# One tile first: the other tiles' first block with tile 0's expert rows between its instructions

## The reference, cut to what matters

```python
h = rms_norm(x, g_mix)
p = h @ w_in                                   # 672 columns for attention, 1792 for the recurrence
y_a = mla_group(p[..., :672], ...)             # w_uq, w_uk, w_uv, norm of q and k, chunk mask, 8 heads
y_r = rwkv7_group(p[..., 672:], ...)           # lora, a state of 64x64 for each of 8 heads, token by token
x = x + concat(y_a, y_r) @ w_o
h = rms_norm(x, g_ffn)
q = (h @ w_pq).reshape(T, 8, 2, 128)           # expert layer, for each block of 128 tokens
s = einsum('thpd,hpnd->thpn', q, sub_keys)
s1, i1 = top_k(s[:, :, 0], 16); s2, i2 = top_k(s[:, :, 1], 16)
top_s, pos = top_k(s1[..., :, None] + s2[..., None, :], 16)    # of the 256 sums
idx = take(i1 * 128 + i2, pos); gate = softmax(top_s)
act = gelu(einsum('thkd,td->thk', expert_u[idx], h))
x = x + einsum('thk,thkd->td', gate * act, expert_v[idx])      # 8 heads x 16 = 128 rows a token
```

## Time and profile before

| what | value |
| --- | --- |
| median of 3 runs | 2452.07 us (2451.54 to 2456.14) |
| profiled execution: span, first to last instruction | 2444.8 us |
| the median less this span | 7.3 us |
| busy: TensorE, VectorE, ACT, GpSimd | 85%, 63%, 48%, 30% of the span |
| moved by DMA | 721.34 MB, mean 295 GB/s |
| granted TensorE clock, mean of the span | 0.910 of full |

### The profile page before, as it was taken

The page is one execution under the profiler, slowest core; times in us unless marked ns, Lnnn a source line. Parts: engine busy times, 40 slices in busy tenths (PEclk is TensorE's granted clock), DMA queues, the critical chain, the costliest instruction groups (busy, mean ns, idle before and its releaser), DMA issues.

```text
span 2444.8 us, 34688 instructions
## 1 busy us (share of the span) xinstructions
PE 2077.5 (85%) x13276; PEld 1613.4 (66%) x13276; DVE 1544.6 (63%) x3434; ACT 1181.8 (48%) x2346; POOL 739.4 (30%) x647
## 2 busy tenths in 40 slices
PE   6989999888868765666659899876998999989998
PEld 4445598678656654555558788755887756858863
DVE  5565676677887746667566787556766544955422
ACT  1123332127776567666676567768776640111110
POOL 2000000004444334555543796333333310800000
PEclk9999879999979987666679999987999999999999
DMA  4321113549999999999999999999999985353441
GB/s 168 121 100 64 70 37 107 182 145 400 421 418 418 415 415 420 422 419 418 415 419 416 412 381 409 414 419 415 400 413 412 411 319 206 112 178 116 167 143 69
DMA packets 158437, 721.34 MB, mean 295 GB/s; under 512 B 10048, under 2 KB 13248, under 8 KB 92224
## 3 DMA queue, kind: packets, MB, share of 16 engines
q0 software_dynamic: 73728, 536.90, 53.5%
q1 hardware_dynamic: 84544, 182.23, 20.5%
HBM read 717.00 MB, written 2.10 MB: 294 GB/s over the span
## 4 chain that ended last, share of the span: by engine, by line
PE 47%; DMA 27%; DVE 13%; ACT 7%; issue 4%; POOL 3%; another core or an unknown queue 0%; SPq 0%; DVEq 0%; POOLq 0%; ACTq 0%
DMA AR<-in_uv,C 24%; PE PA L684 12%; PE PD L1213 8%; PE PA L1146 5%; PE PD L684 5%; ACT AR L1749 3%; PE PA L1159 3%; DVE AR L2635 2%; DMA WR<-in_w_up 2%; POOL AR L2825 2%; PE PD L847 2%; PE PA L1314 2%; PE PD L1314 2%; PE PA L847 1%; DVE AR L2579 1%
## 5 line engine op out<-in xcount | busy, mean ns | idle before, releaser
L2579 DVE CUSTOM_DVE_ANT_0 AR<-AR,HN 128x1024 f32<-128x1024 f32 x512 | 639.6, 1253 | 406.8 <-DMA AR<-in_uv,C 217.3
L2825 POOL DMA_INDIRECT AR<-in_uv,C x512 | 617.4, 1206 | 918.2 <-PE PD L1213 723.0
L1213 PE MATMUL PD<-C,AR 128*128 128x128 f32 x4096 | 653.4, 313 | 279.3 <-ACT AR L1749 278.1
L1213 PEld LDWEIGHTS PD<-C,AR 128*128 128x128 f32 x4096 | 549.9, 162 | 415.1 <-ACT AR L1749 369.0
L1749 ACT ACTIVATE AR<-AR,SC 128x1024 f32<-128x1024 f32 x512 | 588.2, 1149 | 16.7
L1745 ACT ACTIVATE SC<-SC 128x1 f32<-128x1 f32 x512 | 103.3, 202 | 352.1 <-DVE SC L2579 350.7
L684 PE MATMUL PA<-HT,WR 128*128 128x256 f32 (+1 forms) x608 | 185.2, 465 | 1.4 <-ACT AR L1763 1.4
L1146 PE MATMUL PA<-HT,WR 128*128 128x256 f32 x704 | 170.3, 389 | 11.7 <-DMA WR<-in_w_up 11.7
L684 PEld LDWEIGHTS PA<-HT,WR 128*128 128x128 f32 x608 | 116.3, 192 | 64.8 <-issue 55.0
L1747 ACT ACTIVATE SC<-SC,C 128x1 f32<-128x1 f32 x512 | 150.8, 295 | 16.6
L1146 PEld LDWEIGHTS PA<-HT,WR 128*128 128x128 f32 x704 | 131.8, 196 | 28.9 <-DMA WR<-in_w_up 13.3
(11 more groups left out here) (488 smaller groups left out, 2895.4 us busy)
## 6 DMA issues: line engine op xcount, KB each, us to landing
WR<-in_w_up SPq DMA_DIRECT2D x22, 2048.0 KB, 18.3
WR<-in_w_in SPq DMA_DIRECT2D x18, 2048.0 KB, 8.0
WR<-in_w_ada SPq DMA_DIRECT2D x12, 2048.0 KB, 8.3
WR<-in_w_down SPq DMA_DIRECT2D x9, 2048.0 KB, 8.8
WR<-in_w_pq SPq DMA_DIRECT2D x4, 2048.0 KB, 28.8
AR<-in_uv,C POOLq DMA_INDIRECT x512, 14.9
WR<-in_w_out SPq DMA_DIRECT2D x4, 2048.0 KB, 18.1
AR<-in_w_pq SPq DMA_DIRECT2D x3, 2048.0 KB, 10.1
```

The costliest lines, as they stand in the source:

```text
L1213: ins = nc.tensor.matmul(acc[i // 4][:, P * (i % 4):P * (i % 4) + P], uv_row(j, D + P * i, D + P * i + P), ident, start=(k == 0 and i % 4 ...
L2579: ttr(uv_row(j, 0, D), uv_row(j, 0, D), HN[:, t, :], 1.0, 0.0, ALU.mult, ALU.add, DOT[:, j:j + 1]).then_inc(s["dots"], 1)
L2825: nc.gpsimd.indirect_dma_start(uv_row(ring_slot(turn), 0, 2 * D), None, uv, bass.IndirectOffsetOnAxis(ap=IDX[:, t % 2, i:i + 1], axis=0),) ...
```

## The change

The head is run twice: head(FIRST) for tile 0 alone, with tile 0's queries, scores and selection part 0 behind it, and then head(LATE, cut) for tiles 1 to 3. In the second one, 128 places are marked by cut(name); at the k-th, VectorE does the product of tile 0's row k, ACT scales row k-1 and TensorE adds row k-2. Tile 0's selection parts 1 to 3 stand at the late head's beginning (the 18 cuts "sel"), tile 1's part 0 near its end. After the late head TensorE adds what is left of tile 0's rows, and the loop over tiles starts with tile 1, whose rows take over what stood between tile 0's: selection parts 1 to 3 (now tile 1's), the mixing of tiles 2 and 3, their queries (rows 29 to 68) and scores, and tile 2's selection from row 77.

```diff
 def ring_slot(turn):
-    if turn < SEVEN:
-        return turn % 5
-    return (turn - SEVEN) % 7 if turn < EIGHT else (turn - EIGHT) % RING
+    return (0, 1, 8, 9)[turn % 4] if turn < NSEL else turn % RING
...
+BREAKS = [name for name, count in
+          (("sel", 18), ("pm", 3), ("q", 6), ("qkn", 9), ("qkT", 2), ("att", 26), ("lora", 8), ("inv0", 3), ("inv", 15),
+           ("invz", 1), ("chain", 6), ("e1", 2), ("e2", 4), ("e3", 2), ("e4", 2), ("e5", 4), ("e6", 4), ("e7", 13))
+          for _ in range(count)]
...
+            ACC0 = [PA[:, 3, :], PD[:, 3, :]]
+            def first_row(k):
+                j = ring_slot(k)
...
+                pe.wait_ge(s["scaled"], k + 1)
+                for i in range(KD):
+                    ins = nc.tensor.matmul(ACC0[i // 4][:, P * (i % 4):P * (i % 4) + P],
+                                           uv_row(j, D + P * i, D + P * i + P), ident,
...
+            def cut(name, count=1):
+                for _ in range(count):
+                    cuts[0] += 1
+                    if cuts[0] > LAG:
+                        first_row(cuts[0] - 1 - LAG)
...
+            head(FIRST, no_cut)
+            w_mix = head(LATE, cut)
...
+            for k in range(rows_done[0], NSEL):
+                first_row(k)
...
+            def scaled_row(t, k):
...
+                act.wait_ge(s["dots"], turn_ + 1)
+                tell(A(GEL[:, j:j + 1], DOT[:, j:j + 1], ACT.Gelu), "gelu")
...
+            def cut(name, count=1):
+                for _ in range(count):
+                    if cuts[0] > 0:
+                        scaled_row(0, cuts[0] - 1)
+                    cuts[0] += 1
...
+            def product_row(turn_, t):
+                j = ring_slot(turn_)
+                dve.wait_ge(uv_full[j], 16 * ring_uses(turn_))
...
+            def cut(name, count=1):
+                for _ in range(count):
+                    product_row(cuts[0], 0)
+                    cuts[0] += 1
...
-            for t in range(NT):
+            for t in range(1, NT):
                 for k in range(NSEL):
...
+                    if turn == NSEL:
+                        pool.wait_ge(s["a_full"], JA["score", 1, 3] + 1)
```

More of the change, by code:

```diff
@@ L95 @@
 LAG = 2
[L96 to L99, removed]
+MIX_NORM_AT = {2: (5, 8, 11, 14), 3: (16, 18, 21, 23)}
+MIX_TURN_AT = {2: 17, 3: 26}
+QUERY_FROM, QUERY_TO = 29, 68
+SCORE_AT = 70
 def select_at(t):
[L104 removed]
+    return [77 + 5 * i // 4 for i in range(STEPS)] if t == 2 else [15 + 3 * i for i in range(STEPS)]
 GATES_AT = 124
@@ L142, with bank_before @@
 FIRST_A, FIRST_D = {}, {}
-_a = _d = 0
 for _name, _na, _nd in JOBS:
-    FIRST_A[_name], FIRST_D[_name] = _a, _d
-    _a, _d = _a + _na, _d + _nd
-PR_EARLY, PR_IN_ATT = 6, 12
-def pr_after(u):
-    m = PR_EARLY + (u - 2) // 3
-    return m if (u - 2) % 3 == 0 and PR_EARLY <= m < PR_IN_ATT else None
[L160 to L208, removed]
+    FIRST_A[_name], FIRST_D[_name] = len(BANK_A), len(BANK_D)
+    for _i in range(_na):
+        add_a(_name, _i, "late")
+    for _i in range(_nd):
+        if _name == "acc":
+            add_d(_name, _i, "late", bank=_i % 4)
+        else:
+            add_d(_name, _i, "late")
+def bank_before(banks, j):
+    return next((i for i in range(j - 1, -1, -1) if banks[i] == banks[j]), None)
+FIRST_LATE_A = FIRST_A["back0"]
 def query_steps(k):
@@ L525, in build @@
-        chunks.append((1024, w_uv.rearrange("(k p) n -> p k n", p=P), 2, "d", FIRST_D["kv"] + 3))
-        for i in range(2):
-            col_chunk(w_in, MLA_COLS + 512 * i, 512, "a", pr_job(4 * i + 3))
-        for i in (1, 2):
-            col_chunk(w_ada, 512 * i, 512, "a", ada_job(i))
-        for i in (2, 3):
-            col_chunk(w_in, MLA_COLS + 512 * i, (512, 256)[i - 2], "a", pr_job(11) if i == 2 else FIRST_A["lora"] + 11)
-        chunks.append((1024, lora, 1, "a", FIRST_A["lora"] + 11))
@@ L533, in build @@
-        SLOTS += [0, 1, 2, 1, 0, 1, 2, 0, 1, 2, 1, 2, 7]
-        for i in range(3, 12):
-            col_chunk(w_ada, 512 * i, 512, "a", chain_a(3) + 2 if i == 7 else ada_job(i))
-        SLOTS += [0, 1, 0, 1, 0, 1, 1, 1, 2]
-        col_chunk(w_o, 0, 512, "a", FIRST_A["wo2"] + 2)
-        col_chunk(w_o, 512, 512, "a", FIRST_A["last_s"] + 7)
-        SLOTS += [1, 2]
-        col_chunk(w_pq, 0, 512, "a", FIRST_A["second0"] + 3)
-        col_chunk(w_pq, 512, 512, "a", FIRST_A["second1"] + 3)
-        chunks.append((2048, keys, 1, "a", FIRST_A["s"] + 3))
@@ new lines, in _ @@
+            roots(st_a[:, 0:1])
+            act.wait_ge(s["in_const"], 32)
+            b = take("hT", "p")
+            for k in range(4):
+                tell(A(HT[:, k, 0:P], b[:, P * k:P * k + P], ACT.Copy, scale=vv("g_mix", k)), "a_free" if k == 3 else "act")
+            tell(A(csil2, vv("c"), ACT.Silu), "csil")
+            head(FIRST, no_cut)
+            part_exp(0, 0)
+            head(LATE, cut)
+            cut("e6")
+            for t in (2, 3):
+                for k0 in (0, 4):
+                    turned_block(HT, t, k0)
@@ L2238, in select @@
+            angles()
+            head(FIRST, no_cut)
+            for step in range(PART_STEPS):
+                select_part(0, 0, step)
+            gates_part(0, 0)
+            head(LATE, cut)
+            e7 = [(i + 1) * 18 // 13 - 1 for i in range(13)]
+            for step in range(PART_STEPS):
+                select_part(1, 0, step)
+                if step in e7:
+                    cut("e7")
+            gates_part(1, 0)
+            assert cuts[0] == NSEL
             def select(t, step):
```

2499 lines of the change are left out of this document (1430 added, 1069 removed), and 3 rows, old and new, of the table JOBS.

## The result

The changed kernel takes 2573.29 us (median of 4 runs, 2566.63 to 2590.61), the kernel before, measured beside it, 2453.65: a ratio of 1.0497, 95% interval 1.0457 to 1.0538, about 120 us slower. The forecast was 2531, 79 us slower, with a range of 2430 to 2650. The profiled execution took 2575.22 us and has a span of 2573.4.

A forecast was written before the change was run, and what follows sets the result against it. TensorE was taken to bound the head, DMA the row stages. Tile 0 alone 277 plus late head with rows 675 gives 952; less 903, plus 30 inherited, is +79 on 2444.8, plus 7.3 for the runs' median: 2531 us, range 2430 to 2650.

The forecast's parts named there:

- F: Time at which tile 1's first product starts: taken as 903.2 us before the change, forecast 952, break-even 873.
- A: Tile 0 alone, from the start until its first gather: 277 us, with bounds of 235 and 310.
- late block without rows: First block of tiles 1 to 3, run after tile 0's, with none of tile 0's rows in it: 450 us.
- three quarters of each stage: In the late head, tiles 1 to 3 take three quarters of each old four-tile stage, the attention nine tenths.
- On average the ring doesn't set the pace: Tile 0's four gather slots allow a row every 2.6 to 5.0 us, against 5.3 a row in the late head.
- Costing the weights at nothing: Weights reloaded in the late head, about 29 MB, add no time: with the rows 241 GB/s, against 414 reached.
- three signs of being wrong: Late stage with rows at three quarters of the old; tile 0 alone under 200 us; tile 1's stage not above 327.
- Rows hiding: Rival: rows fit in gaps of the late head and only TensorE's 0.9 us each adds; 2431 us, chance 0.15.
- The pile-up: Rival: rows wait in TensorE's or ACT's order and pile up behind the late head; 2626 us, chance 0.03.
- The collision: Rival: weight loads and gathers delay each other in the late head, +60 to 70 us; about 2595 us, chance 0.10.
- The switches: Rival: ACT's 52 table loads in the late attention cost 1.28 us more each, 67; 2598 us, chance 0.03.
- The clock: Rival: waits cut up late TensorE work and its clock falls to a mean of 0.8, +112; 2643 us, chance 0.12.

The follow-up runs named there:

- e1: Changed kernel with tile 0's 128 rows taken out of the late head and put behind it, back to back: 2725.98 us.
- e3: Changed kernel with ACT scaling only 256 of the 1024 columns in tile 0's rows: 2550.32 us.
- e6: Changed kernel with four cuts in tile 0's rows: no Gelu table, a quarter of the scaling, two of eight transposes, an eighth of the product: 2445.52 us.
- e2: Changed kernel with a copy in place of Gelu in tile 0's rows, so ACT need not change tables for them: 2519.84 us.
- e12: Changed kernel with Gelu's tanh form, by small VectorE operations and ACT's Tanh and Identity, in tile 0's rows 37 to 74: 2538.53 us.
- e11: Changed kernel with five ring slots instead of four from tile 0's row 97 on, in the order 1, 8, 9, 0, 6: 2563.39 us.
- e8: Changed kernel with tile 0's gathers bringing 4 KB per token instead of 8: 2540.89 us.
- e13: Changed kernel with the tanh form of e12 in rows 37 to 74 and the five slots of e11 from row 97 on: 2528.93 us.

## Why the prediction came out as it did

The frame held: the time is F plus the old stages, plus what tile 1 inherits. Its terms, forecast and measured:

| term | forecast | measured | by |
| --- | --- | --- | --- |
| A, tile 0 alone | 277 | 253 | windows |
| late block without rows | 450 | 488 | e1 |
| rows outside the attention, 102, and the first landing | 168 + 10 | 188 | e1 against the changed kernel |
| rows in the attention, 26 | 47 | 64 | the same |
| what tile 1's stage inherits | 30 | 33 | windows |

**A.** Cut at the same instructions of VectorE as e1's windows, the stages up to the attention took 82.5 us for 83; attention 24 for 34, lora and inversion 26 for 33, levels 30 for 40, the rest to the selection 68 for 70, selection 23 for 17. That "chains between engines and loads don't shrink" was overdone for the three in the middle.

**The late block without rows.** Selection to attention 132 us (forecast 142), attention 100 (93), lora, inversion and levels 118 (124). The step that failed is "three quarters of each stage" for the last: 136 us for 92 (75 and the last selection part, 17). The chain up to the queries alone takes 100 us, as the old stage did for four tiles, and the end 37 for 17. Tile 1's queries and scores are one tile's work, as tile 0's were in the kernel before, so a quarter less was no price for them; what else makes up the 44 us was not separated. With A's error in the other direction, 277 + 450 - 538 = 189 us were forecast for the split as a whole, and it is 203: near by luck, since errors of -24 and +38 us partly cancel.

**The rows.** The sum came near for the wrong reason. I priced a row at ACT's 1.65 us; e3 shows that 0.64 us less of ACT's part is worth almost nothing outside the attention, and e6 that what its four changes take away together is half of the price. The other half stays with 139 us of waits for gathers; how much of it is the gathers and how much the rows' places in the engines' orders wasn't separated. A row costs 0.7 us in the chain and 2.75 between output norm and queries; 1.65 happened to lie near the mean of 1.84. In the attention the mechanism was the forecast one: ACT is busy 134 of 164 us with loads at each row, and e2 and e12 take 41 and 36 us off the stage. The cost was mis-sized by 17 us, since the forecast took ACT as never waiting. In the changed kernel it waits for TensorE in this stage:

```profile
ACT AR L1692 <- PE PA L867: 25.6, 9, 6.7
```

The Trainium skill (ScalarE: Activation LUTs, What ACT_TABLE_LOAD costs) gives 2.66 us for each switch, the load and a drain. ACT's rows under e2 show the load's 1.28 and 0.02 us before it, so the measurement decides for 1.28; the stage came out 17 us above the forecast, not 72.

**The ring and the weights.** "On average the ring doesn't set the pace" came out (e11: 10 us), but not by its working. A slot's cycle, from a gather's issue to the end of its row's transposes, was put at 10.5 to 19.9 us; over the 128 rows it is 22.4 in the mean, or 5.6 a row, beside a pace of 5.8. The sum left out that a row waits for its turn on each engine: from the product's start to the end of the scaling it takes 7.0 us in the mean, for 2.9 of work, and 4.7 more until its transposes are done, for 0.9. So the four slots are nearly always taken, and in the last two stages VectorE waits 71 us of 174 for gathers. Costing the weights at nothing was right for the block as a whole (231 GB/s) and doubtful at its ends (0.91 and 350 GB/s in the first 90 us), where half the bytes gained 14 and 13 us (e8).

**Tile 1's stage.** 361 us at a DMA share of 1.01, inheriting what stood between tile 0's rows as forecast. None of the three signs of being wrong that the forecast named showed.

The differences of the table, -24 + 38 + 10 + 17 + 3, are 44 us; with 3 for the wrong row of tile 1 and 3 in the later stages that is the distance from 79 to the 129 of the traces.

**The rivals.** Rows hiding: refuted; they add 252 us, and in e6 rows with less than half of their work only reach the old time. The pile-up: refuted by the products' times, and e1 made it on purpose, 2726 us. The collision's 60 to 70 us: not borne out, since half the bytes gave 32 in all; a smaller one stays possible. The switches' 67 us: refuted, the attention came out 17 above the forecast. The clock: 0.84 in the late block, but 0.87 without rows, 0.86 in A, and 0.94 up to the first gather before; it fell with the split more than with the rows, lora's 0.63 being 0.61 without rows. How much of the split's 203 us is clock was not separated, so this rival is not refuted.

**Left open.** Moving rows from the end into the levels and the chain, where a row costs 0.7 to 1.05 us, was not tried: it needs more places to cut, or two rows in one. An estimate from the table above is some 18 rows by at most 2 us, 36 us; with e13's 2529 it would not reach 2453.

## What to carry to other kernels

A stage that is limited by DMA can be hidden in one that isn't, but ask first what it costs to make the hiding place: here running one tile ahead cost 203 us, with the work that had stood between the rows, while the stage to be hidden was worth 362 us, less 33 that its neighbour inherits, 3 in later stages and 252 that the rows cost in their new place: 74. Price a visitor between another stage's instructions by that stage, not by its longest part: 0.7 to 2.75 us for the same row. Count a buffer's cycle with the turns that its user waits for in the other engines' orders, not with the work alone: 22.4 us here, for 10.5. And look which tables ACT holds on both sides of it: a function from the host's own set (Tanh beside Exp) took 35 us off without touching the order.

## What the hardware showed that I had not expected

- Taking work from TensorE made a stage longer: with two of eight transposes the late attention went from 164 to 173 us, while its granted clock went from 0.88 to 0.73; taking ACT's table loads away raised the clock of the same stage to 0.94 to 0.96 with all of TensorE's work in it.
- Rows back to back with four slots, and nothing else to do (e1), ran at a clock of 0.55 and 3.15 us a row, with the DMA engines at 0.91.
- Halving a gather's bytes changed its best landing from 5.4 to 4.0 us, not by half.
